# Depthwise taps on TensorE by 64-channel halves, with weights sliced from a band of diagonals in DRAM

## What is computed

```python
h = rms_norm(x, norm_g)
u = h @ pw1_w + pw1_b
u = u[..., :D_MODEL] * jax.nn.sigmoid(u[..., D_MODEL:])
u = causal_depthwise_conv(u, dw_w, dw_b)          # width 31, each channel by itself
u = jax.nn.silu(layer_norm(u, ln_g, ln_b))        # mean and variance over the 1024 channels
x = x + u @ pw2_w + pw2_b
```

## Time and profile before

| | |
|---|---|
| median of 3 runs | 1284.3 us (1284.09 to 1289.94) |
| the profiled execution: its own time | 1283.49 us |
| span of its records | 1281.7 us |
| granted TensorE clock over the span | 0.991 |
| busy: PE, DVE, ACT, POOL | 1238.3, 843.0, 544.3, 111.2 us |

### The profile page before, as it was taken

The page is one execution under the profiler, slowest core; times in us unless marked ns, Lnnn a source line. Parts: engine busy times, 40 slices in busy tenths (PEclk is TensorE's granted clock), DMA queues, the critical chain, the costliest instruction groups (busy, mean ns, idle before and its releaser), DMA issues.

```text
span 1281.7 us, 16583 instructions
## 1 busy us (share of the span) xinstructions
PE 1238.3 (97%) x6085; PEld 1021.3 (80%) x6085; DVE 843.0 (66%) x1158; ACT 544.3 (42%) x942; POOL 111.2 (9%) x99
## 2 busy tenths in 40 slices
PE   6998997999999999999999999997999999999999
PEld 4787756788888888887998889966888888888887
DVE  7999946577627763676577777665577537762673
ACT  6256955444314431345454545433444324431441
POOL 4000001200000000002324141401200000000000
PEclk9999998999999999999999999998999999999999
DMA  5221001222322222223221212211222322232222
GB/s 212 81 91 59 1 5 53 98 76 98 109 89 98 98 99 99 81 74 109 96 70 34 67 34 67 66 33 33 99 94 91 111 69 96 98 118 79 99 74 91
DMA packets 16615, 104.00 MB, mean 81 GB/s; under 512 B 1840, under 2 KB 1968, under 8 KB 5424
## 3 DMA queue, kind: packets, MB, share of 16 engines
q1 hardware_dynamic: 16560, 103.25, 24.2%
HBM read 101.15 MB, written 2.10 MB: 81 GB/s over the span
## 4 chain that ended last, share of the span: by engine, by line
PE 89%; DVE 6%; ACT 3%; POOL 1%; issue 1%; DMA 0%; SPq 0%; POOLq 0%; DVEq 0%; ACTq 0%
PE bank L1034 67%; PE bank L1152 9%; PE bank L1088 5%; PE bank L1184 2%; PE bank L1214 2%; POOL sq_sum L415 1%; DVE w_lo L707 1%; DVE w_lo L699 1%; ACT prob L661 1%; DVE prob L980 1%; PE bank L1105 1%; PE bank L1187 1%; DVE prob L982 1%; PE bank L1079 1%; DMA w_raw<-stream 0%
## 5 line engine op out<-in xcount | busy, mean ns | idle before, releaser
L1034 PE MATMUL bank<-xg_hi,w_hi 128*128 128x512 f32 x832 | 326.8, 393 | 13.6 <-DVE xg_lo L715 11.1
L1034 PE MATMUL bank<-xg_lo,w_hi 128*128 128x512 f32 x832 | 325.0, 391 | 0.0
L1034 PE MATMUL bank<-xg_hi,w_lo 128*128 128x512 f32 x832 | 325.0, 391 | 0.0
L470 ACT ACTIVATE w_hi<-w_raw 128x2048 fp32r<-128x2048 f32 x83 | 158.3, 1907 | 156.5 <-PE bank L1034 156.5
L699 DVE TENSOR_TENSOR w_lo<-w_raw,w_hi 128x2048 fp32r<-128x2048 f32 x83 | 192.6, 2320 | 30.9 <-ACT w_hi L470 30.9
L1034 PE MATMUL bank<-act_hi,w_hi 128*128 128x512 f32 x480 | 193.2, 402 | 8.9 <-DVE act_lo L831 7.2
L1034 PEld LDWEIGHTS bank<-xg_hi,w_hi 128*128 128x128 f32 x832 | 156.9, 189 | 48.3 <-DVE w_lo L730 11.1
L1034 PE MATMUL bank<-act_lo,w_hi 128*128 128x512 f32 x480 | 190.8, 398 | 0.0
L1034 PE MATMUL bank<-act_hi,w_lo 128*128 128x512 f32 x480 | 190.6, 397 | 0.0
L604 ACT ACTIVATE ffn_t<-ffn_u,par 128x512 f32<-128x512 f32 x88 | 72.0, 818 | 268.6 <-DVE ffn_u L884 268.6
L1034 PEld LDWEIGHTS bank<-xg_lo,w_hi 128*128 128x128 f32 x832 | 157.0, 189 | 33.3 <-issue 0.7
(11 more groups left out here) (141 smaller groups left out, 1607.6 us busy)
## 6 DMA issues: line engine op xcount, KB each, us to landing
w_raw<-stream SPq DMA_DIRECT2D x87, 1024.0 KB, 4.9
w_raw<-stream SPq DMA_DIRECT2D x8, 768.0 KB, 4.3
x<-x_t SPq DMA_DIRECT2D x8, 256.0 KB, 6.8
out_t<-x SPq DMA_DIRECT2D x8, 256.0 KB, 2.0
w_raw<-stream SPq DMA_DIRECT2D x2, 512.0 KB, 5.1
par<-params SPq DMA_DIRECT2D x1, 345.5 KB, 2.9
lam_in<-lambdas SPq DMA_DIRECT2D x1, 128.0 KB, 8.6
```

Source lines behind the costliest of these rows:

```text
L470: act.activation(w_hi[:, j, :], w_raw[:, j, :], ACT.Copy).then_inc(w_hi_done, 1)
L1034: got = pe.matmul(out, weights(w, j, k, m), v[:, k, :], start=(k == 0 and s == 0), stop=(k == count - 1 and s == 2), skip_group_check=True)
```

## The change

The lists become `DVE_TILES = [0, 1, 2, 3]` and `PE_TILES = [4, 5, 6, 7]`. DVE has 124 tap instructions left; 72 of them are in the pw1 loop as before.

PE treats a channel tile as two halves of 64 channels. A matmul takes 64 rows (channels of the half h) and 128 output columns: the first 64 are the channels at odd positions, the other 64 the same channels at even positions. Its moving operand is every second position of `u` (256 columns). Column block t of the weights holds the diagonal of tap t-1, so that the slice of blocks t and t+1 gives position 2p+1 its tap t-1 and position 2p its tap t. 32 offsets cover all taps, two more blocks hold the bias, which is multiplied by `ones_r`. That makes 32 x 2 x 3 + 4 = 196 matmuls of 64 rows by 256 columns a tile, the half h=0 and the half h=1 by turns, each into a bank of its own. One tile is finished before the next begins.

The weights are not made by ACT any more. A tensor `band` in DRAM (4 tiles x 128 x 2240) is filled by SP: one DMA a tile writes zeros into it (1.15 MB each), then three small DMAs a tile write 31 tap weights and twice the bias into each row, 128 runs of 124 and of 4 bytes. Each row is then a strip of 64 x 35 elements. It is loaded like a weight unit (units 8 to 11; pw2 moves to 12 to 15) and split like one by ACT and DVE, which read it with a step of 35 elements (140 bytes) and write it block by block (`split_band`).

ACT brings the result from the two banks to `conv_c` in four copies of 64x256, written at every second position. `VAR` moves to bank 6. DVE clears `zeros` (128x2240) and sets `ones_r` at the start.

```diff
@@ PE @@
+            def taps(i):
+                n = FIRST["taps"] + i
+                j = n % RING
+                pe.wait_ge(w_lo_done, n + 1)
+                if i < RING:
+                    pe.wait_ge(banks_free, n + 1)
+                else:
+                    pe.wait_ge(pe_tile, i - RING + 1)
+                pe.wait_ge(u_lo_done, i + 1)
+                for s, (w, u) in enumerate(((w_hi, u_hi), (w_hi, u_lo), (w_lo, u_hi))):
+                    for t in range(OFFSETS):
+                        at = t * HD
+                        for h in range(2):
+                            rows = slice(h * HD, (h + 1) * HD)
+                            pe.matmul(bank[2 * j + h][:, 0:SEQ // 2], w[rows, j, at:at + P], u[rows, i, t:t + SEQ - 1:2],
+                                      start=(s == 0 and t == 0), stop=False, skip_group_check=True)
...
+            for i, m in enumerate(PE_TILES):
+                taps(i)
+                if i < len(DVE_TILES) - 1:
+                    pe.wait_ge(c_done, i + 1)
+                    mean(DVE_TILES[i], start=i == 0)
+                if i:
+                    pe.wait_ge(pe_tile, i)
+                    mean(PE_TILES[i - 1])
+            pe.wait_ge(pe_tile, len(PE_TILES))
+            mean(PE_TILES[-1])
+            pe.wait_ge(c_done, len(DVE_TILES))
+            mean(DVE_TILES[-1], stop=True).then_inc(mean_mm, 1)
@@ ACT @@
+            for i, m in enumerate(PE_TILES):
+                n = FIRST["taps"] + i
+                act.wait_ge(tiles, TILE0 + 2 * n + 2)
+                for h in range(2):
+                    for e in range(2):
+                        got = act.activation(conv_c[h * HD:(h + 1) * HD, m, e:SEQ:2],
+                                             bank[2 * (n % RING) + h][(1 - e) * HD:(2 - e) * HD, 0:SEQ // 2], ACT.Copy)
+                got.then_inc(pe_tile, 1)
+                split_next(n + 2)
             fetch_table(ACT.Sqrt)
@@ DVE @@
-            dve.wait_ge(dw_hi_done, 1)
-            dve.tensor_tensor(dw_lo, par[:, PARAM_AT["dw_w"]:PARAM_AT["dw_w"] + KT * TAPS], dw_hi.bitcast(F32),
-                              sub).then_inc(dw_lo_done, 1)
...
+            for n in range(KT + 1, FIRST["pw2"] + 1):
+                split_next(n)
+                convolve(16)
             convolve(len(taps))
@@ SP @@
+            sp.wait_ge(pad_done, 5)
+            for n in range(RING, KT, RING):
+                for j in range(RING):
+                    sp.wait_ge(w_lo_done, n + j - RING + 1)
+                    sp.dma_start(w_raw[:, j, 0:SLOT], stream[:, STARTS[n + j]:STARTS[n + j + 1]]).then_inc(w_in[j], 16)
+                for i in ((0,), (1,), (2, 3))[n // RING - 1]:
+                    sp.dma_start(bass.AP(band.tensor, i * P * STRIP, [[STRIP, P], [1, STRIP]]), zeros
+                                 ).then_inc(band_zero, 16)
+            sp.wait_ge(band_zero, 16 * len(PE_TILES))
...
+            sp.wait_ge(band_set, 48 * len(PE_TILES))
```

More of the change, by code:

```diff
@@ L86, in unit_plan @@
     phase("pw1", KT)
+    phase("taps", len(PE_TILES), STRIP)
     phase("pw2", KT // 2)
@@ L91, in unit_plan @@
     ffn(1)
-    starts = [sum(widths[:n]) for n in range(len(widths) + 1)]
+    streamed = [0 if first["taps"] <= n < first["pw2"] else width for n, width in enumerate(widths)]
+    starts = [sum(streamed[:n]) for n in range(len(widths) + 1)]
     return first, widths, starts
@@ L235, in trunk @@
         conv_u, at = put("conv_u", conv_area, [P, KT, CP])
-        diag, at = put("diag", at, [P, DIAGS, len(PE_TILES), 2, P], F32R)
+        ones_r, at = put("ones_r", at, [P, SEQ // 2], F32R)
+        zeros, at = put("zeros", at, [P, STRIP])
         assert at <= area
@@ L243, in trunk @@
         u_lo, at = put("u_lo", at, [P, len(PE_TILES), CP], F32R)
-        dw_hi, at = put("dw_hi", at, [P, KT * TAPS], F32R)
-        dw_lo, at = put("dw_lo", at, [P, KT * TAPS])
         lam_in, at = put("lam_in", at, [P, 4, HD])
@@ L469, in split_weights, with split_band, split_next @@
                 act.wait_ge(tiles, TILE0 + 2 * n - 2)
-                act.activation(w_hi[:, j, :], w_raw[:, j, :], ACT.Copy).then_inc(w_hi_done, 1)
+                act.activation(w_hi[:, j, 0:SLOT], w_raw[:, j, 0:SLOT], ACT.Copy).then_inc(w_hi_done, 1)
+            def split_band(n, j):
+                act.wait_ge(w_in[j], (n - j) * (16 // RING) + 16)
+                act.wait_ge(tiles, TILE0 + 2 * n - 2)
+                act.activation(w_hi[:, j, :].rearrange("p (t c) -> p t c", c=HD),
+                               w_raw[:, j, :].rearrange("p (c t) -> p t c", c=HD), ACT.Copy).then_inc(w_hi_done, 1)
+            def split_next(n):
+                (split_band if FIRST["taps"] <= n < FIRST["pw2"] else split_weights)(n, n % RING)
             def split_gained(n, parts):
@@ L698, in split_weights, with split_band, split_next @@
                 dve.wait_ge(w_hi_done, n + 1)
[L699 removed]
+                dve.tensor_tensor(w_lo[:, j, 0:SLOT], w_raw[:, j, 0:SLOT], w_hi[:, j, 0:SLOT].bitcast(F32),
+                                  sub).then_inc(w_lo_done, 1)
+            def split_band(n, j):
+                dve.wait_ge(w_hi_done, n + 1)
+                by_tap = "p (t c) -> p t c"
+                dve.tensor_tensor(w_lo[:, j, :].rearrange(by_tap, c=HD), w_raw[:, j, :].rearrange("p (c t) -> p t c", c=HD),
+                                  w_hi[:, j, :].rearrange(by_tap, c=HD).bitcast(F32), sub).then_inc(w_lo_done, 1)
+            def split_next(n):
+                (split_band if FIRST["taps"] <= n < FIRST["pw2"] else split_weights)(n, n % RING)
             def split_gained(n, parts):
@@ L1079, in mean @@
                 return pe.matmul(bank[NORM][:, :], ones[:, :], conv_c[:, m, :], start=start, stop=stop, skip_group_check=True)
-            pe.wait_ge(pad_done, 3)
-            for t in range(TAPS):
-                for n, m in enumerate(PE_TILES):
-                    if t == 0:
-                        pe.wait_ge(u_lo_done, n + 1)
-                    pe.wait_ge(diag_done, len(PE_TILES) * t + n + 1)
-                    for s, (w, u) in enumerate(((0, u_hi), (0, u_lo), (1, u_hi))):
-                        got = pe.matmul(bank[CONV[n]][:, :], diag[:, t % DIAGS, n, w, :], u[:, n, t:t + SEQ],
-                                        start=(t == 0 and s == 0), stop=(t == TAPS - 1 and s == 2), skip_group_check=True)
-                    got.then_inc(diag_used, 1)
-                if t in MEAN_AFTER:
-                    pe.wait_ge(c_done, MEAN_AFTER[t] + 1)
-                    mean(MEAN_AFTER[t], start=MEAN_AFTER[t] == 0)
@@ L1096, in _ @@
-            pe.wait_ge(c_done, 4)
-            mean(3)
-            for n, m in enumerate(PE_TILES):
-                pe.wait_ge(pe_tile, n + 1)
-                mean(m)
-            pe.wait_ge(c_done, 5)
-            mean(4, stop=True).then_inc(mean_mm, 1)
+            def taps(i):
+                n = FIRST["taps"] + i
+                j = n % RING
[12 more added lines that the diff above has]
+                                      start=(s == 0 and t == 0), stop=False, skip_group_check=True)
+                for w in (w_hi, w_lo):
+                    for h in range(2):
+                        rows = slice(h * HD, (h + 1) * HD)
+                        got = pe.matmul(bank[2 * j + h][:, 0:SEQ // 2], w[rows, j, STRIP - P:STRIP], ones_r[rows, :],
+                                        start=False, stop=w is w_lo, skip_group_check=True)
+                        if w is w_lo:
+                            got.then_inc(tiles, 1)
```

71 lines of the change are left out of this document (31 added, 40 removed).

## The result

| | before | after |
|---|---|---|
| median | 1287.1 us (4 runs, 1284.1 to 1291.6) | 1319.0 us (4 runs, 1318.1 to 1320.7) |
| profiled execution, and its span | 1283.5, 1281.7 us | 1318.1, 1316.3 us |
| granted clock over the span | 0.991 | 0.980 |
| first subtraction of the mean on DVE | 183.60 | 210.82 |
| from there to the end of the span | 1098.1 | 1105.5 |

The ratio is 1.0246, with an interval of 1.0207 to 1.0286: slower. The forecast of 1267 us, and its range up to 1312, both missed. Of the 34.6 us between the two spans 27.2 arise before the first subtraction. The pair of halves cost 0.231 us, and 0.2 or above was the prediction's own sign of being wrong.

What follows compares the result with a forecast made beforehand. PE bounds the kernel, its taps setting the first mean subtraction at 183.6; that would come at 166.1, 17.5 us earlier, less 0.8 for ACT's split: -16.7 against 1283.5 gives 1267 us, range 1263 to 1275, 8 in 10 within 1263 to 1312.

Steps and rivals of the forecast that it cites:

- the prediction's own sign of being wrong: PE's taps: the forecast is wrong if a pair of half-array matmuls is at 0.2 us or above.
- The pair: PE's taps: two 64-row, 256-column matmuls on different halves overlap wholly, at 0.127 us a pair.
- the term of 49.8 us for four tiles: PE's taps: four tiles of 98 pairs at 0.127 us each, 49.8 us.
- The rival "one after another": PE's taps: halves don't overlap, 94.1 us in place of 49.8, mean at 210.4, 1311 us in all; chance 0.38.
- Start at 106.3: PE's first tap matmul comes at 106.3, right behind pw1, without the wait of 4.7 us.
- the rival "strided splits": Strip splits on ACT and DVE cost double; DVE ends at 171.3, 1273 us; within the 0.46 for 1263 to 1275.
- the contiguous price: Strip splits reading with a step of 140 bytes cost 2.1 us on ACT and 2.5 on DVE, as contiguous.
- Sums and changes of height: PE after tiles 4, 5 and 6: sums of 0.86 us and changes of 0.35, together 1.6, 2.4 and 2.4.
- The end: After PE's last tap: ACT's four copies at 0.45 us (1.8), two sums and 0.1, together 3.6 us.
- The new piece: Behind the stage: ACT splits a unit (1.9 us) between the last copy and the root's table, costing 0.8.
- DVE done at 157.3: DVE ends its taps and strip splits at 157.3, four us before PE ends its last tile at 162.5.
- the late band's 177.7: Rival: small band writes end at 105, not 94; mean at 177.7, 1279 us; chance 0.16 together with partial overlap.

Runs made afterwards that it cites:

- two planes: The changed kernel with u_hi and u_lo stored as even and odd positions apart, so the moving operand is 256 neighbouring columns: 1277.3 us, ratio to before 0.9933.
- plain ones: The changed kernel with its four strips split by contiguous reads and writes (not the convolution wanted): 1310.7 us.
- the strip turned: The kernel with two planes, ACT making u_hi before strip splits and copying each strip tap by tap into the place of zeros: 1273.5 us, ratio 0.9910.

## Why the prediction was wrong, point by point

**The pair: right on the overlap, wrong in price, by a term that was put at nothing.** The forecast took whole overlap at 0.127 a pair, and the halves do overlap: 0.119 with two planes. The step that failed is the term of 49.8 us for four tiles. It took the earlier trace rows, all at unit step, as the price of 256 columns at a step of two, and put that step at nothing (the sentence under the rivals that PE's step of two would be free). Such a matmul costs 0.2285 alone, and the pair 0.231, so four tiles took 89.9 us, not 49.8: +40.1. None of the rivals had this cause.

The Trainium skill, "SBUF — State Buffer", section Specifications (TRN2), cachelines, asks for two hits in a 16-byte line for full bandwidth. By that rule a step of 8 bytes is free. ACT's and DVE's reads of `conv_u` with this step agree nearly (ACT 0.65 to 0.67 us against 0.61 to 0.63, DVE 0.69 as before); PE's moving operand does not, and the measurement decides. For the step of 140 bytes the page names a penalty, and the splits show one.

**The rival "one after another"** put the first subtraction at 210.4; it came at 210.82. It was right by accident: the pair cost 0.231 for another reason, and its errors cancelled (tiles 4.2 less than its 94.1, sums 1.5 less, the start 5.9 more).

**Start at 106.3.** It was 112.19: +5.9. The strip lay ready at 100.6, not 99, for which 0 to 2 us were allowed; leaving out the small writes gives back 2.8. The zeros were not what was late: they had landed by 83.1, where 85 was forecast. The splits were dear (the rival "strided splits"): plain ones give back 4.5. The reason given for the contiguous price, that 0.9 elements a ns is the pace of all DVE rows, did not hold even there: a tap of 512 elements has 0.78 (0.66 us). And behind both stood what no term had: ACT makes `u_hi` after the split, in order, so DVE's wait of 5.09 grows with it.

**Sums and changes of height.** 4.9 us in place of 6.4: a change costs less than the 0.35 assumed. **The end** after the last tap was 3.84 against 3.6; ACT's four copies took 1.6 against 1.8. **The new piece** of ACT's split before the root cost 0.5 against 0.8: the first square followed 1.23 us after the first subtraction, 0.72 before.

The stage by these: 166.1 + 5.9 + 40.1 - 1.5 + 0.2 = 210.8.

**DVE done at 157.3.** With PE at its forecast pace (two planes) it was 170.9 (172.30 less 1.37): 7.1 us of waiting for `u_hi` that the stream had no place for, and four splits that cost some 1.8 more each, 7.2; with these the sum comes to 171.6. The rival's 171.3 was the better number. It did not decide the outcome, since PE was far behind. Two sums of the prediction are off by a little and change nothing: DVE at 157.3 is 5.2 us, not four, ahead of PE's 162.5, and the late band's 177.7 gives 1278, not 1279.

**The range.** Its upper end of 1312 had the right stage and the profiled execution's 1098.1 behind it, the fastest of all profiles. The 17 runs of before beside the kernel with two planes spread from 1282.3 to 1291.7. A range built on one run at the fast end had to reach some 8 us higher.

With the step of two undone, the forecast's version exists: 1277.3, and 1273.5 with the strip turned, against 1267 forecast.

## What to carry to other kernels

Price a matmul by rows with its own access pattern, not only its shape: a step of two in the moving operand made 256 columns as dear as 512. Store the operand in planes when it is written; here ACT and DVE paid next to nothing for the step. Two 64-row matmuls on different halves of the array do cost one, but only by turns.
Give a forecast the spread of the part that the change does not touch: here it was 10 us, as much as several of the effects looked for.
When the bound moves, follow every wait of the engine that is next: here an order on ACT, a strip's arrival and a dear split each hid behind the other.

## What the runs showed of the hardware

- A 128x256 fp32r matmul whose moving operand has a step of two elements: 0.2285 us and a latency of 0.41, against 0.12 and 0.28 at unit step, at the full clock. Other steps and other types were not run.
- 64-row matmuls on the two halves by turns: 0.119 a pair at 256 columns, 0.234 at 512; on one half in succession 0.114 for each single one.
- With one half of the rows in use at a time the granted clock was 0.50, the 1.2 GHz level, over the first two tiles (112 to 190 us). Behind two full-height sums it was 0.95 with two planes (190 to 239), but 0.54 with the step of two (190 to 284), with as many matmuls of the same shape. What decides it is open.
- At a granted clock of 0.64 a pass of 64 matmuls at unit step took 5.72 us against 3.81 at 1.00; at a step of two 7.45 at 0.68 against 7.32.
- ACT and DVE over 128x2240 with a read step of 140 bytes: 4.43 and 4.22 to 4.42 us, against 2.08 and 2.48 contiguous; a step of 8 bytes over 512 elements cost ACT some 0.04 us (0.65 against 0.61) and DVE nothing (0.69).
- Zeros from SBUF to DRAM, 1120 KB: 8.8 us to landing, but each was issued right behind a load of 1024 KB (4.9 in the median) or another such write, so most of that is waiting in the queue. The load of unit 7 and the two writes behind it, 3.3 MB, were issued by 72.6 and had landed by 83.1, when the small writes began; these held SP for 9.15 us. The page's line on the zeros, and SP in order of time:

```profile
band<-zeros SPq DMA_DIRECT2D x4, 1120.0 KB, 8.8
```

```profile
83.07 9.15 SPq L382 DMA_DIRECT2D band<-params  x12
```
